# Other slot order and other buffers in a differential attention, and paired steps in a windowed attention

## The reference, cut to what matters

```python
# layer 0: differential attention, 8 heads, 256 context + 1024 latent tokens
s = einsum('bqhmd,bkhmd->bhmqk', qb, keys) * ATTN_SCALE      # m = 0, 1: two maps
p = softmax(s, axis=-1)
a = p[:, :, 0] - lam * p[:, :, 1]
o = einsum('bhqk,bkhe->bqhe', a, vals)
# latent queries see all 1280 keys, context queries the 256 context keys alone
# then o is normed over its 128 columns, gated and multiplied by w_o

# layer 1: windowed attention, 16 heads in 4 groups, per 128 queries
s = [q @ k_context (256 keys), q @ k_band (up to 384 keys, masked)]
p = softmax([s, sink])[..., :-1]
o = p @ v
```

## Time and profile before

| | |
|---|---|
| median of three runs | 3048.55 us |
| the profiled execution | 3043.0 us |
| its span, first to last instruction | 3040.9 us |
| mean granted TensorE clock | 0.975 of full speed |
| TensorE matmul busy | 2850.8 us (94%) |
| TensorE weight load busy | 2390.3 us (79%) |
| VectorE / GpSimd / ScalarE busy | 1749.1 / 1041.6 / 985.2 us |
| DMA | mean 84 GB/s |

### The profile page before, as it was taken

The page is one execution under the profiler, slowest core; times in us unless marked ns, Lnnn a source line. Parts: engine busy times, 40 slices in busy tenths (PEclk is TensorE's granted clock), DMA queues, the critical chain, the costliest instruction groups (busy, mean ns, idle before and its releaser), DMA issues. The chain is left out here.

```text
span 3040.9 us, 43601 instructions
## 1 busy us (share of the span) xinstructions
PE 2850.8 (94%) x16380; PEld 2390.3 (79%) x16380; DVE 1749.1 (58%) x2531; ACT 985.2 (32%) x1741; POOL 1041.6 (34%) x643
## 2 busy tenths in 40 slices
PE   7989999999999999999989988888889798999998
PEld 6778787778888888788878878878778587777776
DVE  5634453765555455567766258788743792077743
ACT  4122461311111111231111137677731201277731
POOL 3433313655444555423322212223243352211231
PEclk9989999999999999999999999999999899999999
DMA  6544621111111111023354321212011142431111
GB/s 195 178 135 138 149 64 49 56 42 55 48 48 41 48 48 55 21 90 131 128 180 152 121 95 62 87 54 93 21 37 42 42 152 83 138 95 46 29 42 70
DMA packets 214042, 255.67 MB, mean 84 GB/s; under 512 B 9386, under 2 KB 182639, under 8 KB 213887
## 3 DMA queue, kind: packets, MB, share of 16 engines
q1 hardware_dynamic: 198306, 190.14, 21.0%
q10 hardware_dynamic: 15584, 63.51, 5.3%
HBM read 188.02 MB, written 65.60 MB: 83 GB/s over the span
## 5 line engine op out<-in xcount | busy, mean ns | idle before, releaser
L1045 PE MATMUL ps<-hh,w_parts 128*128 128x512 f32 (+2 forms) x2560 | 980.5, 383 | 43.4 <-POOL w_parts L819 24.4
L1046 PE MATMUL ps<-hl,w_parts 128*128 128x512 f32 (+2 forms) x2560 | 974.5, 381 | 0.0
L1047 PE MATMUL ps<-hh,w_parts 128*128 128x512 f32 (+2 forms) x2560 | 970.2, 379 | 0.0
L817 POOL TENSOR_TENSOR w_parts<-w_raw,zero 128x1024 fp32r<-128x1024 f32 x140 | 293.1, 2093 | 920.0 <-PE ps L1047 683.5
L1045 PEld LDWEIGHTS ps<-hh,w_parts 128*128 128x128 f32 x2560 | 488.4, 191 | 141.3 <-issue 30.8
L1047 PEld LDWEIGHTS ps<-hh,w_parts 128*128 128x128 f32 x2560 | 487.2, 190 | 92.3
L1046 PEld LDWEIGHTS ps<-hl,w_parts 128*128 128x128 f32 x2560 | 488.5, 191 | 89.3 <-issue 0.7
L819 POOL TENSOR_TENSOR w_parts<-w_raw,w_parts 128x1024 fp32r<-128x1024 f32 x140 | 346.3, 2474 | 11.0
L1971 ACT ACTIVATE f_y<-f_z,convv 128x1024 f32<-128x1024 f32 x44 | 54.8, 1246 | 507.4 <-DVE f_z L2543 507.2
L2745 DVE TENSOR_SCALAR_CACHE_REDUCE b_s<-ps 128x640 f32<-128x640 f32 (+1 forms) x128 | 100.0, 781 | 94.2 <-PE ps L1604 94.0
L2543 DVE TENSOR_TENSOR f_z<-ps,f_rs 128x1024 f32<-128x1024 f32 x44 | 53.8, 1224 | 170.7 <-PE ps L1047 170.6
(11 more groups left out here) (358 smaller groups left out, 4782.6 us busy)
## 6 DMA issues: line engine op xcount, KB each, us to landing
w_mod_sb<-in_w_mod SPq DMA_DIRECT2D x16, 1536.0 KB, 7.1
w_raw<-in_w_up SPq DMA_DIRECT2D x44, 512.0 KB, 3.9
w_raw<-in_a_w_in SPq DMA_DIRECT2D x32, 512.0 KB, 4.1
d_raw<-in_w_down SPq DMA_DIRECT2D x22, 512.0 KB, 4.2
w_raw<-in_w_in SPq DMA_DIRECT2D x20, 512.0 KB, 5.4
za_parts<-z_hi ACTq DMA_DIRECT2D x16, 640.0 KB, 3.0
za_parts<-z_lo ACTq DMA_DIRECT2D x16, 640.0 KB, 4.1
d_even<-za_parts SPq DMA_DIRECT2D x16, 640.0 KB, 6.5
```

The lines of the kernel that those rows point to most:

```text
L817: pool.tensor_tensor(wh[:, s], w_raw[:, s], zero[:].broadcast_to([P, KT * P]), ALU.add).then_inc(w_high[s], 1)
L1045: pe.matmul(out_, w_hi, x_hi, start=start, stop=False)
L1046: pe.matmul(out_, w_hi, x_lo, start=False, stop=False)
L1047: return pe.matmul(out_, w_lo, x_hi, start=False, stop=stop)
```

## The change

Differential attention: the loop over pairs of heads is written out on all engines; a step is named by one number n. The slots of the inner heads take the tiles in the order 2, 3, 4, 5, 6, 0, 7, 8, 1, 9, those of the last head in the order 2, 3, 4, 5, 6, 0, 7, 8, 9, 1; the first head keeps 0 to 9. All buffers of the second map are now tiles of their own. Where the scores of slot u + 2 are short, TensorE mixes slot u - 1 directly after them, ahead of the wait for the weighed maps. GpSimd no longer waits for VectorE's last weighing before it splits the first output weights.

Windowed attention: TensorE works two steps at a time: turn, scores, scores, turn, then the spread and two or three tiles of the mix. ScalarE copies the turned tiles of every fourth step ahead of the spread reciprocals.

```diff
+DA_FIRST = tuple(range(DA_UNITS))
+DA_INNER = (2, 3, 4, 5, 6, 0, 7, 8, 1, 9)
+DA_LAST = (2, 3, 4, 5, 6, 0, 7, 8, 9, 1)
+DA_RING0, DA_RING1 = 3, 2
...
-        d_p1 = [w_areas[0][:, TOK:2 * TOK], alloc(scope, "d_p1", [P, TOK])[:]]
+        d_p1 = [alloc(scope, f"d_p1{s}", [P, TOK])[:] for s in range(2)]
-        d_p1s = [w_areas[0][:, 2 * TOK + u * CTX:2 * TOK + (u + 1) * CTX] for u in range(2)]
+        d_p1s = [alloc(scope, f"d_p1s{s}", [P, CTX])[:] for s in range(2)]
...
-            pool.wait_ge(da_weighed, 3 * (10 * DA_HEADS - 1))
             pool.wait_ge(da.mixed, 10 * (DA_HEADS - 1) + 1)
             split(pool, W0["a_out"], 0, 0)
...
+            for n in range(DA_HEADS * DA_UNITS):
+                h, u = divmod(n, DA_UNITS)
+                short = False
+                if n + LEAD < DA_HEADS * DA_UNITS:
+                    da_scores(n + LEAD)
+                    short = da_context(n + LEAD)
+                if short and n:
+                    da_mix(n - 1)
+                pe.wait_ge(da_weighed, 3 * n + 3)
+                for k in range(len(batches(da_tiles(n)))):
+                    if k == 2 and n and not short:
+                        da_mix(n - 1)
+                    da_turn_map(n, k)
+                if da_context(n) and n and not short:
+                    da_mix(n - 1)
+                if u in DA_OUT and h:
+                    da_turn_output(h - 1, u - DA_OUT[0])
...
-BA_MIX = ((0,), (1, 2), (3,), (4,))
+BA_MIX = ((0, 1, 2), (3, 4))
-            for u in range(BA_UNITS + 4):
-                if u + BA_LEAD < BA_UNITS:
-                    ba_scores(u + BA_LEAD)
+            for u in range(0, BA_UNITS + 4, 2):
                 if u < BA_UNITS:
                     ba_turn(u)
+                for z in range(2):
+                    if u + BA_LEAD + z < BA_UNITS:
+                        ba_scores(u + BA_LEAD + z)
+                if u < BA_UNITS:
+                    ba_turn(u + 1)
                 if u < BA_UNITS and u % 4 == 2:
                     ba_spread(u // 4)
                 if u >= 4:
-                    for n in BA_MIX[u % 4]:
+                    for n in BA_MIX[u % 4 // 2]:
                         ba_mix(u // 4 - 1, n)
...
             for u in range(BA_UNITS):
                 b, a = divmod(u, 4)
-                if a == 3:
-                    ba_rows(b)
                 act.wait_ge(ba_turned[0], u + 1)
...
                 act.activation(b_pt[:, b % 2, 0:3, a], ...).then_inc(ba_copied[0], 1)
+                if a == 3:
+                    ba_rows(b)
```

More of the change, by code:

```diff
@@ L52, in batches, with da_slots, da_tile, da_context @@
     return [range(n, min(n + 4, blocks)) for n in range(0, blocks, 4)]
[L55 to L83 removed]
+DA_UNITS = TOK // P
+DA_FIRST = tuple(range(DA_UNITS))
+DA_INNER = (2, 3, 4, 5, 6, 0, 7, 8, 1, 9)
+DA_LAST = (2, 3, 4, 5, 6, 0, 7, 8, 9, 1)
+DA_RING0, DA_RING1 = 3, 2
+def da_slots(h):
+    return DA_FIRST if h == 0 else DA_LAST if h == DA_HEADS - 1 else DA_INNER
+def da_tile(n):
+    return da_slots(n // DA_UNITS)[n % DA_UNITS]
+def da_context(n):
+    return da_tile(n) < CTX // P
+def da_tiles(n):
+    return CTX // P if da_context(n) else TOK // P
+def da_place(n):
+    return sum(not da_context(v) for v in range(n))
+def da_user(n, ring):
+    alike = [v for v in range(n) if (da_tile(v) == da_tile(n) if da_context(n) else not da_context(v))]
+    back = 1 if da_context(n) else ring
+    return alike[-back] if len(alike) >= back else None
+def da_outputs_of(h, k):
+    return max(da_slots(h)[u] // 4 for u in batches(DA_UNITS)[k])
+def da_plan():
+    turns = []
+    for n in range(DA_HEADS * DA_UNITS):
+        turns += [("p", n, k) for k in range(len(batches(da_tiles(n))))]
+        h, u = divmod(n, DA_UNITS)
+        if u in DA_OUT and h:
+            turns.append(("o", h - 1, u - DA_OUT[0]))
+    turns += [("o", DA_HEADS - 1, k) for k in range(3)]
+    return {key: divmod(n, 2)[::-1] for n, key in enumerate(turns)}
+def da_turn(*key):
+    return da_plan()[key]
+def da_turned_by(n):
+    return sum(len(batches(da_tiles(v))) for v in range(n + 1))
 def da_order(width):
@@ L1508, in da_scores @@
                     if m == 0 and c == 2 * BANK and turn == 0:
-                        pe.wait_ge(da_bank_left, 16 * j + (8 * e + u - 1))
-                    ins = pe.matmul(got, q[r, u * P:(u + 1) * P], k[r, c:c + w], start=(turn == 0), stop=(turn == 2))
-                    if m == 1 and c == 0 and turn == 2 and u >= 2:
+                        pe.wait_ge(da_bank_left, da_place(n) + 1)
+                    ins = pe.matmul(got, q[r, tile], k[r, c:c + w], start=(turn == 0), stop=(turn == 2))
+                    if m == 1 and c == 0 and turn == 2 and not da_context(n):
                         ins.then_inc(da_bank_left, 1)
@@ L1527, in da_mix, with da_turn_output @@
                 last.then_inc(da.mixed, 1)
-            def da_turn_output(j, e, k):
+            def da_turn_output(h, k):
                 if k == 0:
[L1531 to L1554, removed]
@@ L2025, in da_keep_out, with da_keep_turned @@
[L2025 to L2030, removed]
+                act.activation(p, p, ACT.Exp, bias=d_low[:, u, m:m + 1], scale=-1.0, accum_out=d_sum[:, h % 2, m, u:u + 1]).then_inc(done, 1)
+            def da_keep_turned(n, k):
+                blocks = batches(da_tiles(n))[k]
+                b, before = da_turn("p", n, k)
+                act.wait_ge(da_turned, da_turned_by(n - 1) + k + 1)
+                act.activation(d_pt[n % 2][:, blocks.start:blocks.stop], bank(6 + b)[:, 0:len(blocks) * P].rearrange("p (k q) -> p k q", q=P),
+                               ACT.Copy).then_inc(da_free[b], 1)
@@ L2630, in da_max @@
                 dve.wait_ge(da.scored, n + 1 + 1)
                 dve.tensor_scalar(p0, ps[:, 0:w], -SCALE, HIGHEST, ALU.mult, ALU.min, accum_out=d_low[:, u, 0:1]).then_inc(da.maxed, 1)
-                if u >= 4:
-                    dve.wait_ge(da_weighed, 3 * n - 3)
-                elif not first:
-                    dve.wait_ge(da_weighed, 60 * j + (30 * e - 30 + (3 * u + 3 if u < 2 else 30)))
+                if weighed is not None:
+                    dve.wait_ge(da_weighed, 3 * weighed + 3)
```

270 lines of the change are left out of this document (130 added, 140 removed).

## The result

| | before | after |
|---|---|---|
| median of seven runs | 3046.68 us | 3063.38 us |
| lowest and highest | 3039.61, 3051.45 | 3058.01, 3069.58 |
| the profiled execution | 3043.0 us | 3069.58 us |
| its span | 3040.9 us | 3067.8 us |
| mean granted TensorE clock | 0.975 | 0.964 |

After to before, the ratio is 1.006, 95% interval 1.005 to 1.007: the change makes the kernel slower by 0.6%. I had predicted 3043.5 and a range of 3020 to 3058; the time lies outside it, 19.9 us above the forecast.

What follows compares the result with a forecast made beforehand. TensorE was taken as the bound, busy 0.9 or more in most slices. Differential attention +18.7 and windowed -23.5 gave -4.8 us: 3038 against the profiled execution, 3043.5 against the median; range 3020 to 3058.

Steps and rivals of the forecast that it cites:

- Clean inner heads: Differential attention, heads 1 to 6 without low clock: 47.0 us of work and 10.3 of waits, 57.3 each.
- The clock: TensorE's low clock after the 2.2 and 3.7 us waits: 1.6 us added per inner head, between 0 and 3.4.
- First and last head: Differential attention's outer heads: first +1.6 us from full scores in slots 8 and 9, last -1.5.
- rival 3: Lower clock costs 5.1 us an inner head, not 1.6: stage +40, total +16, 3065 us; chance 0.07.
- Rival 2: The clock stays up after the inner heads' waits: stage +9, total -15, 3034 us; chance 0.22.
- The port: Slot 7 of inner heads: VectorE's weighing loses to GpSimd's splits, so TensorE waits 3.7 us where 1.5 was.
- the row at 2131.62: Earlier trace row: VectorE's weighing, 0.02 us ahead of a GpSimd instruction, still took 0.63, 0.14 over its usual.
- Rival 1: VectorE's weighing goes ahead of GpSimd's second split: inner head 54.5, total -26, 3022 us; chance 0.15.
- Windowed attention: Pairing steps saves TensorE joints, 0.86 us per four steps, 28 fours: -23.5 us, bounds -12 and -27.
- Rival 4: Windowed joints are a modelling artefact or the turn waits for banks; gain under 5: total +13, 3062 us; chance 0.06.
- Written-out loop: Differential attention: writing out the loop removes 3.0 us of issue at its turn, held in the old 55.8 per head.
- Rival 5: Instruction fetch of the longer program costs some us more: 3050 us; chance 0.05.

Runs made afterwards that it cites:

- run 4: Changed kernel, with GpSimd's two splits in heads 1 to 6 held until slots 7 and 8 are weighed: 3027.7 us.
- run 3: Changed kernel plus idle transposes in heads 1 to 6, 20 ahead of slot 3's moved mix and 28 ahead of slot 7's weighed maps: 3043.4 us.
- run 7: Changed kernel with all heads in the old slot order 0 to 9 and no mix moved ahead: 3026.1 us.
- run 6: Changed kernel with GpSimd's splits held until slots 7 and 8 are weighed, and slot 2's full mix back behind slot 3's turns: 3018.8 us.
- run 11: Changed kernel plus 28 idle transposes in the slot 7 wait of heads 1 to 6, none in slot 3: 3053.5 us.
- run 2: Kernel before the change with only the windowed attention's change added: 3025.6 us, ratio to before 0.9932.
- run 9: Changed kernel with the old slot order, no mix moved ahead, and GpSimd's splits held until slots 7 and 8 are weighed: 3021.7 us.
- run 1: Changed kernel with the windowed attention as before, so the differential attention's change alone: 3082.6 us, ratio to before 1.0115.
- run 10: Changed kernel with later GpSimd splits, slot 2's mix back behind slot 3's turns, and 8 idle transposes ahead of slot 3's maps in heads 1 to 6: 3012.8 us.
- both repairs: Changed kernel with GpSimd's splits held until slots 7 and 8 are weighed, and slot 2's full mix back behind slot 3's turns.
- run 8: Changed kernel with later GpSimd splits and 20 idle transposes ahead of slot 3's moved mix in heads 1 to 6: 3022.5 us.
- run 12: Changed kernel with later splits, slot 2's mix back and slot 3 idle transposes, plus idle transposes at three places of the last head: 3012.3 us.

## Why the prediction was wrong

**Clean inner heads: 57.3 forecast, 58.2 measured.** The waits were right one by one (9.6 us in those above, forecast 10.1; a bracket counts from the modelled end of the matmul before, so the waits do not add up with prices from start to start). The order of limits was walked rightly too: the same slots and the same releasers. The 0.9 are in small terms, read in a quiet head of run 4: the moved mix starts 0.3 later, the turns behind it take 0.2 more, the weighed maps of slot 6 come 7.14 us behind their scores and not 6.95, and scores held by VectorE's maxima come 5.2 us after the last ones and not 5.14. Six heads: 5.4 us. Without a low clock in the inner heads the change would have been about even (run 3: 3043.4; that this is the forecast of 3043.5 is luck, since the forecast had some low clock in it and the heads 0.9 shorter).

**The clock: this is the step that failed.** It stood as "With a wait of 2.2 (half of the time) and one of 3.7 (nearly always; ...) I add 1.6 a head". Run 3 shows 3.2: in the kernel after both waits are followed by a stretch in every inner head, and each costs 1.6, not 1.2. The 3.2 lie inside the term's own bounds (0 to 3.4), but alike in six heads they take the total out of the range. The price of a stretch was off by a third: 1.2 is what it costs in the old order (56.3 against 55.1 in run 7), 1.5 to 1.7 in the new one (runs 3, 4 and 6). The larger error was in how often. I took four of eight as a chance of one half and averaged it over six heads. Six heads with the same waits at the same places are not six draws. In the kernel after all did the same; in most other runs the heads with a low stretch stood in a row (the first four of six in run 4, the first three in run 6, the first alone in run 11, the second and third in the kernel before, the first two and the last in runs 2 and 9). Run 7 is not so neat: all but the second. The excess of 1.6 is 9.6 us in heads 1 to 6. First and last head came 1.6 and 2.2 above their terms, at a lower clock too (0.86 where it was 0.91 before the change, 0.91 where it was 0.95); for the first head other runs bear this out, since the same head took 59.3 and 59.2 us at 0.91 in runs 1 and 10, where the forecast had 59.0; for the last head it is read from the trace, and no run shows it alone. Together 13.4 of the 18.7 us that the stage missed; the other 5.4 are the clean heads. The mechanism is near that of rival 3, though no stretch was twice as long (its 5.1 a head were too many, and that its 3065 came so near is luck). Its bound was "slower from 3.9 us a head": measured are 3.2, and 0.9 of work beside it, 4.1 above the same 57.3. I gave it 0.07. Rival 2, the clock staying up, is out: all 12 such waits of the kernel after were followed by a low stretch.

**The port: right.** L2676 lost to the split that it was stamped 0.02 us ahead of, as the row at 2131.62 had said, and run 4 shows that moving GpSimd's work takes the wait away. By the wording of the Trainium skill, page "SBUF — State Buffer", section "Who interferes with whom", that the second to issue is the one blocked, the wait would have been 1.0; the stamps here show the first one blocked, at that distance. Rival 1 is out. What the pair cost was 3.42 us and a low stretch, not the wait alone: run 4 was worth 35.7 us by the medians, of which the wait is 6 x 3.5 = 21 and eight low stretches fewer are 13.

**Windowed attention: -18.7 for -23.5.** Between the first and the last spread the pairing gives 21.2; at the ends another 0.8. In a full group the joints give 0.78 (8.97 to 8.19), forecast 0.86, and in most of the others 0.38 to 0.85. Of the forecast's 23.5 that leaves some 1.5 unfound, within the sum of the joints. The rest is at the start: first scores to first spread took 11.7 us before, 15.0 in the kernel after and 11.2 in run 2, with waits at the turns of 3.6, 4.8 and 2.4. Rival 4 is out.

**Written-out loop:** "The 55.8 holds what goes: 3.0 us of issue" was right of the trace, and worth nothing in time: run 7 is as fast as run 2, with two low stretches more. Rival 5 is out; no issue wait stood in its heads.

**Profile and medians.** Between the spans of the profiled executions the change costs 26.9 us, between the medians 16.7. The kernel before was profiled 3.7 below its later median of 3046.7, the one after 6.2 above its own. So of the 31.7 us that the profiled executions lie beside the -4.8 of the forecast, 18.7 are the differential attention, 4.8 the windowed one and 8.2 stretches that the change does not touch; the medians lie 21.5 beside it.

## What to carry to other kernels

Price a wait on TensorE as the wait and, as a second case, a stretch of low clock behind it; and reckon it for all equal turns and for none, not for an average share of them: here neighbouring turns mostly did the same, and in the kernel after all twelve waits. Where one engine of a pair that shares a port has slack, place its work beside what reads PSUM on the other: two waits on GpSimd were worth 35.7 us in the changed kernel and 4.4 in the old order (run 9), where the new order itself, with both repairs, is worth 1.0 us a head. Time that cannot be filled with work can be filled with idle transposes at no cost if they end before the wait does: runs 3, 8 and 10 gained 20.0, 5.2 and 6.0 us by them; run 12, in the last head, gained nothing.

## What the runs showed of the hardware that was not expected

- The low clock (0.50, 3.4 us at a time, 1.5 to 1.7 us lost each in the new order) follows waits of 1.1 and 0.6 us close together (run 6) as it follows 3.42; and after the same 2.42 it came in the kernel after and not in five heads of run 11, after the same 3.42 not in one head of run 1.
- A VectorE instruction of one column (L2673, 0.22 us) took 1.64 behind GpSimd's split, and the 1.55 us one right after it took 4.27: between two splits that follow each other within 0.1 us VectorE did not get its turn for the large one, in any of the six inner heads.
- The wait at the windowed attention's second turn varied from 1.2 (run 7) to 3.7 us (the kernel after) between kernels whose code there is the same.
